# A two-block layer on one core: SBUF operands moved to PSUM, the head norm moved to VectorE, a second S5 buffer, a reordered opening, and each head's value product one tile later

## The chip, the cores and the metric

One NeuronCore of a Trainium2 chip runs the whole program. The time is the device time in microseconds (us). The kernel before took 3418.79 us, the median of three runs (3416.71 to 3423.25).

## What is computed

A residual stream `x` of 256 tokens by 2048 channels (f32) passes through two transformer blocks. The change touches the first block's token mixer alone:

```
mod = silu(c) @ w_ada + b_ada                       # shifts, scales, gates: 96 columns of 128
h = rmsnorm(x) * (1 + sc) + sh                      # the opening needs the first 32 columns
q, k, v, g_ret, u, gate_r, gate_s = split(h @ w_in)
q, k = rope(q), rope(k) * 128**-0.5                 # 8 heads, q and k of 128, v of 256
scores = (q k^T) * decay                            # causal, 256 x 256 per head
ret = head_group_norm(scores v)                     # mean and variance over the 256 of a head
y_ret = (silu(g_ret) * ret) @ w_ret_out
y_ssm = gelu(s5(u))                                 # 64 groups, complex diagonal scan over time
y = sigmoid(gate_r) * y_ret + sigmoid(gate_s) * glu(y_ssm @ w_s5_glu)
```

## The kernel before, in words

Everything is laid out feature by token: a tile is 128 features by 256 tokens. A matrix product of the first mixer takes one **weight tile** (128 output features, 16 slices of 128 by 128) and makes 48 matmuls of 256 columns, three for each slice (high part of the weights times high and low part of the activations, low part times high part: L636 to L638). Four ring slots hold weight tiles. SyncE loads the raw tile when the slot is free (L554), ScalarE copies it to the high part (L1006), VectorE subtracts for the low part (L1490, `split_lo`), TensorE multiplies. `ahead` on ScalarE and VectorE handles the tile two products ahead. Every engine works through its queue in the order of the code.

The stages that matter, in order of time:

- **Opening** (`modulation_rows`, `value_weights`, `row_pair`, `heads_values`). For each of the 16 channel tiles k VectorE reduces two rows of `w_ada`, 1 MB each (shift row k and scale row 16 + k, L1512), forms `normed`, and ScalarE adds the shift. TensorE then makes 16 matmuls of 512 columns (L730) that accumulate the values of all heads in all eight PSUM banks. SyncE issues the loads: value weights for two k at a time (2 MB in 8 loads, runs of 1 KB), then the rows of these two k.
- **u** (8 weight tiles, products of `u`).
- **heads** (32 weight tiles, four per head: q, k and the two halves of the gate; r is the tile's place in the head, n counts heads). Beside each tile run steps of the head before. After tile r = 0 TensorE makes the head's **value product** `ret_values` (scores times v, L753 to L755), for which VectorE must have masked the scores (`ret_masked`, L1750). At r = 1 VectorE takes the statistics of `p_o` and ScalarE the root; at r = 2 VectorE computes scale and shift (`ret_scale`, L1743, L1744), ScalarE writes the normed head (`ret_normed`, L1172), VectorE rotates q and k (`rotate`, L1763 to L1768). At r = 3 TensorE makes the scores of the new head and transposes the normed one (`ret_back`, L761), and ScalarE copies the gate product out of PSUM (`ret_g`). In the next head's r = 0 VectorE multiplies by the gate (`ret_out`, L1723), gates (`ret_gated`, L1755) and splits (`ret_done`, L1729).
- **ret** (32 weight tiles, four iterations g of eight, m = 0 to 7). For m of 0 to 3 ScalarE evacuates a gate; for m of 4 to 7 it copies the product to `val_a` or `val_b`, and VectorE multiplies it into `m_ret` (L1830). The first iteration also carries the last head's steps. From the second on VectorE reduces a late row of `w_ada` at m = 0, 3 and 6 (`aside_z`).
- **S5** runs through heads and ret: at every even m TensorE makes a product into `p_z`; one tile later VectorE turns it (L1696, L1697), adds (L1699, L1700) and scans twice (L1702, L1703) in `s5_w`; GpSimd turns it back (L2215 to L2218) into `s5_x`. VectorE waits with a new tile until GpSimd has finished the one before (`scan_done`).
- glu, out1 and the second half (feed-forward, second block) follow, and are not touched.

Of the kernel before, what the change touches and what calls it, by code (L numbers as in the profile page):

```python
# [137 lines left out]
def stages():  # L138
# [3 lines left out]
    ph["heads"] = Phase(4, [(W, KT)] * 8, 0)  # L142
    for name in ("u", "ffa", "att"):
        ph[name].opens = True
        ph[name].opening_lo = 4 if name == "u" else 3
# [56 lines left out]
def program(nc, dram, out):  # L202
    stored, ph = schedule(), stages()
    with ExitStack() as ctx:
# [13 lines left out]
        with ExitStack() as shared:  # L218
# [3 lines left out]
            s5_w = sb(shared, "s5_w", [P, 2, T])  # L222
            s5_v = sb(shared, "s5_v", [P, 2, T])
# [22 lines left out]
        with ExitStack() as block1:  # L246
            c_act = sb(block1, "c_act", [P, D])
            with ExitStack() as mixer:
# [42 lines left out]
                with ExitStack() as retention:  # L291
                    aside_r = sb(retention, "aside_r", [P, D])
                    qk_sin = sb(retention, "qk_sin", [P, 2, T])
                    qk_rot = sb(retention, "qk_rot", [P, 2, T])
                    g_t = sb(retention, "g_t", [P, 2, T])
# [5 lines left out]
                    gn_shift = sb(retention, "gn_shift", [P, 2])  # L301
# [90 lines left out]
        def bank(name):  # L392
# [3 lines left out]
        p_turn, p_score, p_o, p_norm, p_z, p_y = (bank(n) for n in ("p_turn", "p_score", "p_o", "p_norm", "p_z", "p_y"))  # L396
        v_banks = acc + [p_turn, p_score, p_o, p_norm, p_z, p_y]
# [29 lines left out]
        R = {n: sem("ret_" + n) for n in ("qk", "rope", "g", "decay", "scored", "masked", "gated", "summed", "var",  # L427
                                          "std", "scale", "normed", "back", "tanh", "out", "hi", "done")}
# [81 lines left out]
        def _(sp):  # L510
# [10 lines left out]
            def modulation_rows(k):  # L521

                for j, row in enumerate((k, KT + k)):
# [6 lines left out]
            def value_weights(two):  # L530

                quad, part = divmod(two, 2)
                if two == 2:
                    sp.wait_ge(c_set, 1)
                if quad >= 2:
                    sp.wait_ge(v_step, 4 * (quad - 2) + 2 * part + 2)
                for n in range(4):
                    for half in range(2):
                        at = stored["heads"].offsets[V_BLOCK[n // 2]]
                        src = dram["w_heads"][2 * (n % 2) + half, at:at + 2 * KT * P * P].rearrange(  # L540
                            "(j p c) -> p j c", j=2, p=P)[:, :, 2 * P * two:2 * P * (two + 1)]
                        dst = wv[quad % 2][n][:, 2 * half:2 * half + 2, 2 * part:2 * part + 2, :].rearrange("p j k c -> p j (k c)")
                        sp.dma_start(dst, src).then_inc(wv_in[quad % 2][part], 16)  # L543

            modulation_rows(0)
            for two in range(KT // 2):
                value_weights(two)
# [1859 lines left out]
```

## Time and profile before

| | |
|---|---|
| median of 3 runs | 3418.79 us |
| lowest, highest | 3416.71, 3423.25 us |
| the profiled execution, its own time | 3422.44 us |
| its span in the trace | 3420.7 us |
| mean granted TensorE clock | 0.99 |
| busy: TensorE, VectorE, ScalarE, GpSimd | 97%, 69%, 43%, 13% of the span |

Busy shares are means over stages with different limits. How to read the sections below: a row of a timeline gives the start and the duration in us, the engine and line, what is written and read, and in square brackets how long the engine sat idle before it and what ended that. A matmul's duration runs past the start of the next one, since matmuls are pipelined; the start to start distance is what one costs.

### The profile page before, as it was taken

To read this page: it belongs to the slowest core of one execution; us is meant where nothing else is said; L and a number is where in the kernel's file an instruction comes from. 1 tells how busy PE (TensorE), PEld (TensorE's weight loads), DVE (VectorE), ACT (ScalarE), POOL (GpSimd) and SP (SyncE) were. 2 spreads that over 40 slices of the span, in tenths; PEclk is the share of its full clock that TensorE was granted. 3 is DMA by queue.
4 is the path that set the end of the run, shared out by engine and by line. 5 is a ranking of instruction groups with operands and counts; after the bars stand their busy time and mean duration, and the time that the engine had idled before them with its cause. 6 is when DMAs were issued, how large, how long until landed. Compare 5 with 4: busy or idle time off the path is not lost.

```text
span 3420.7 us, 52032 instructions
## 1 busy us (share of the span) xinstructions
PE 3321.5 (97%) x20368; PEld 2945.6 (86%) x20368; DVE 2356.8 (69%) x2479; ACT 1469.3 (43%) x1504; POOL 431.8 (13%) x309
## 2 busy tenths in 40 slices
PE   7999999999989999999989999999999999999998
PEld 3599999899978888888878888888888888888887
DVE  6689988877676666656666567657677766666554
ACT  2256565444444444433354443443434444444332
POOL 1036677700200000000000000000002100000000
PEclk9999999999999999999999999999999999999999
DMA  9874455578735555567724444555555555555554
GB/s 380 346 306 173 165 184 216 203 302 307 265 134 186 194 185 193 186 246 265 259 99 169 164 162 180 187 185 190 186 194 190 185 193 187 190 190 182 192 190 147
DMA packets 126274, 706.34 MB, mean 206 GB/s; under 512 B 14160, under 2 KB 41424, under 8 KB 47840
## 3 DMA queue, kind: packets, MB, share of 16 engines
q1 hardware_dynamic: 115808, 695.96, 55.1%
q10 hardware_dynamic: 10368, 9.02, 0.8%
q8 instruction: 68, 1.11, 0.1%
q14 instruction: 30, 0.25, 0.0%
HBM read 702.83 MB, written 2.10 MB: 206 GB/s over the span
## 4 chain that ended last, share of the span: by engine, by line
PE 82%; DVE 8%; DMA 2%; POOL 2%; issue 2%; SPq 2%; ACT 1%; DVEq 0%; ACTq 0%; POOLq 0%
PE acc L639 44%; PE acc L640 24%; PE acc L636 4%; PE acc L638 4%; PE acc L637 4%; DVE ring_lo L1490 2%; SPq L543 1%; DVE ring_raw L1512 1%; DMA ring_raw<-w_ada 1%; DMA s_c_sb<-s_c 1%; POOL s_x L2215 1%; POOL s_w L2216 1%; PE p_norm L685 1%; ACT ring_hi L1006 0%; POOL s_prod L2225 0%
## 5 line engine op out<-in xcount | busy, mean ns | idle before, releaser
L639 PE MATMUL acc<-h_split,ring_hi 128*128 128x512 f32 x4736 | 1656.0, 392 | 9.2 <-DVE h_split L1552 4.5
L1490 DVE TENSOR_TENSOR ring_lo<-ring_raw,ring_hi 128x2048 fp32r<-128x2048 f32 (+2 forms) x560 | 1266.2, 2263 | 545.2 <-ACT ring_hi L1006 544.4
L640 PE MATMUL acc<-h_split,ring_lo 128*128 128x256 f32 x4736 | 1337.6, 282 | 0.0
L1006 ACT ACTIVATE ring_hi<-ring_raw 128x2048 fp32r<-128x2048 f32 (+2 forms) x560 | 1040.0, 1861 | 410.2 <-DMA ring_raw<-w_down 150.4
L639 PEld LDWEIGHTS acc<-h_split,ring_hi 128*128 128x128 f32 x4736 | 891.8, 188 | 197.4 <-issue 9.7
L640 PEld LDWEIGHTS acc<-h_split,ring_lo 128*128 128x128 f32 x4736 | 897.9, 190 | 0.4
L639 PE MATMUL acc<-ffn_split,ring_hi 128*128 128x512 f32 x1408 | 488.2, 390 | 0.0
L2157 POOL TENSOR_TENSOR sq_sum<-sq_sum,tile 128x256 f32<-128x256 f32 x60 | 76.5, 1275 | 2570.6 <-ACT tile L1032 2570.6
L640 PE MATMUL acc<-ffn_split,ring_lo 128*128 128x256 f32 x1408 | 397.1, 282 | 0.0
L636 PE MATMUL acc<-h_split,ring_hi 128*128 128x256 f32 x1152 | 329.9, 286 | 10.4 <-DVE ring_lo L1490 7.5
L637 PE MATMUL acc<-h_split,ring_hi 128*128 128x256 f32 x1152 | 323.8, 281 | 0.0
L638 PE MATMUL acc<-h_split,ring_lo 128*128 128x256 f32 x1152 | 323.6, 281 | 0.0
L639 PEld LDWEIGHTS acc<-ffn_split,ring_hi 128*128 128x128 f32 x1408 | 264.3, 188 | 55.4
L640 PEld LDWEIGHTS acc<-ffn_split,ring_lo 128*128 128x128 f32 x1408 | 266.1, 189 | 0.0
L636 PEld LDWEIGHTS acc<-h_split,ring_hi 128*128 128x128 f32 x1152 | 218.9, 190 | 13.2 <-issue 6.5
L637 PEld LDWEIGHTS acc<-h_split,ring_hi 128*128 128x128 f32 x1152 | 218.8, 190 | 0.8 <-issue 0.2
L638 PEld LDWEIGHTS acc<-h_split,ring_lo 128*128 128x128 f32 x1152 | 218.8, 190 | 0.0
L1323 ACT ACTIVATE ffn_split<-ffn_a 128x256 f32 (+1 forms) x88 | 36.8, 419 | 361.8 <-DVE ffn_a L1914 361.8
L1505 DVE TENSOR_REDUCE ffn_b<-acc 128x256 f32<-128x512 f32 x88 | 60.8, 691 | 144.1 <-PE acc L640 144.0
L1032 ACT ACTIVATE tile<-x_res 128x256 f32 (+1 forms) x80 | 33.0, 417 | 152.1 <-DVE x_res L2138 84.7
L2215 POOL TENSOR_TENSOR s_x<-s_w,s_tab 128x512 f32<-128x512 f32 x32 | 88.5, 2765 | 53.0 <-DVE s_w L1703 50.1
L1321 ACT ACTIVATE ffn_t<-ffn_a 128x256 f32<-128x256 f32 x88 | 36.8, 418 | 130.0 <-DVE ffn_a L1910 119.3
(384 smaller groups left out, 3993.1 us busy)
## 6 DMA issues: line engine op xcount, KB each, us to landing
ring_raw<-w_ff SPq DMA_DIRECT2D x88, 1024.0 KB, 4.8
ring_raw<-w_down SPq DMA_DIRECT2D x64, 1024.0 KB, 4.8
ring_raw<-w_ffb SPq DMA_DIRECT2D x56, 1024.0 KB, 4.8
ring_raw<-w_mix SPq DMA_DIRECT2D x48, 1024.0 KB, 4.8
ring_raw<-w_ada SPq DMA_DIRECT2D x32, 1024.0 KB, 10.8
ring_raw<-w_heads SPq DMA_DIRECT2D x32, 1024.0 KB, 4.8
ring_raw<-w_ret SPq DMA_DIRECT2D x32, 1024.0 KB, 5.2
ring_raw<-w_glu SPq DMA_DIRECT2D x32, 1024.0 KB, 5.0
```

The source lines that it names most:

```text
L636: mm(dst[:, 0:T], hi[s][:, t, :], moving[:, k, 0:T], start=start, stop=False)
L637: mm(dst[:, 0:T], hi[s][:, t, :], moving[:, k, T:], start=False, stop=False)
L638: return mm(dst[:, 0:T], lo[s][:, t, :], moving[:, k, 0:T], start=False, stop=stop)
L639: mm(dst[:], hi[s][:, t, :], moving[:, k, :], start=start, stop=False, skip_group_check=True)
L640: return mm(dst[:, T:], lo[s][:, t, :], moving[:, k, 0:T], start=False, stop=stop, skip_group_check=True)
L1006: run(hi[s][:, 0:n, :], raw[s][:, 0:n, :], COPY).then_inc(hi_done, 1)
L1321: run(t[i % 2][:], a[i % 2][:], ACT.Tanh, scale=0.5).then_inc(f_tanh, 1)
L1323: run(dst[:, 4 * g + (first + i), 0:T], a[i % 2][:], COPY, scale=0.5).then_inc(f_hi, 1)
L1490: tt(lo[s][:, 0:n, :], raw[s][:, 0:n, :], hi[s][:, 0:n, :], SUB).then_inc(lo_done, 1)
L1505: v.tensor_reduce(dst, acc[o % 2][:].rearrange("p (c t) -> p t c", c=2), AX_X, ADD).then_inc(sum_done, 1)
L2157: tt(sq_sum[:], sq_sum[:], tile[b][:], ALU.add).then_inc(sq_used, 1)
L2215: tt(xs[:], s5_w[:], sin, ALU.mult)
```

## The change

1. **PSUM operands.** `qk_sin` (the rotated part, then each head's gated result) moves from SBUF to the bank of `p_turn`. The copy `g_t` of the gate product disappears: ScalarE's Tanh and VectorE's `ret_gated` read the product's bank, and TensorE waits for `gated` where it waited for the copy. In S5 the second turned product is written in place in `p_z`, and `s5_v` disappears. In ret the products m = 4 to 7 are read by VectorE in their bank; ScalarE's copy to `val_a`, `val_b` disappears, and a new function `ret_bank` makes TensorE wait for VectorE (`m_done`) before it reuses such a bank.
2. **Norm.** VectorE writes the normed head (subtract the mean, multiply by the inverse root) in two operations, in place of its small shift operation and ScalarE's two.
3. **S5 buffers.** `s5_w` is doubled; VectorE waits for the tile before the last.
4. **One tile later.** `ret_values` goes from r = 0 to r = 1, the statistics and the root from r = 1 to r = 2, the norm from r = 2 to r = 3.
5. **Opening.** Value weights are loaded for four k at a time (runs of 2 KB) and for the last four k in two loads of two; the scale row comes before the shift row; `normed` is formed between the two rows.

```
-                for j, row in enumerate((k, KT + k)):
+                for j, row in enumerate((KT + k, k)):
...
-            for two in range(KT // 2):
-                value_weights(two)
-                for k in range(max(1, 2 * two), 2 * two + 2):
+            for first, n in ((0, 4), (4, 4), (8, 4), (12, 2), (14, 2)):
+                value_weights(first, n)
+                for k in range(max(1, first), first + n):
                     modulation_rows(k)
...
-                    pe.wait_ge(*((R["g"], n) if some(n) else (evac_done, ph["u"].outs * ph["u"].iters)))
+                    pe.wait_ge(*((R["gated"], n) if some(n) else (evac_done, ph["u"].outs * ph["u"].iters)))
...
-                    if r == 0 and some(n):
+                    if r == 1 and some(n):
                         ret_values(n, n - 1)
...
+            def ret_bank(p, g, m):
+
+                if 2 <= m < 6:
+                    return evac_done, p.out_count(g, m - 2)
+                if opening(g) and m < 2:
+                    return (R["gated"] if m else R["qk"]), HEADS
+                return m_done, 4 * g + (m - 1 if m < 2 else m - 5)
...
-            def row_pair(k):
-
-                p, first = ph["ada"], 2 * (k % 2)
-                for j in (first, first + 1):
-                    ada(raw[j][:].rearrange("p k c -> p (k c)"), raw_in[j], slot_free[j], p.uses(k // 2, j), j)
-                for j in (first, first + 1):
-                    dve.wait_ge(slot_free[j], p.uses(k // 2, j))
-                at = slice(k, k + KT + 1, KT)
-                own.step(stt(mod[:, at], ada_sum[:, first:first + 2], 0.5, b_ada[:, at], MUL, ADD))
-                own.step(stt(gain[:, 0, k:k + 1], mod[:, KT + k:KT + k + 1], 1.0, gains[:, 0, k:k + 1], ADD, MUL))
+            def first_row(k, j, at):
+
+                p, slot = ph["ada"], 2 * (k % 2) + j
+                ada(raw[slot][:].rearrange("p k c -> p (k c)"), raw_in[slot], slot_free[slot], p.uses(k // 2, slot), slot)
+                dve.wait_ge(slot_free[slot], p.uses(k // 2, slot))
+                return stt(mod[:, at:at + 1], ada_sum[:, slot:slot + 1], 0.5, b_ada[:, at:at + 1], MUL, ADD)
...
             for k in range(KT):
-                row_pair(k)
+                own.step(first_row(k, 0, KT + k))
+                own.step(stt(gain[:, 0, k:k + 1], mod[:, KT + k:KT + k + 1], 1.0, gains[:, 0, k:k + 1], ADD, MUL))
                 if k == 0:
                     inverse_std(1)
-                stt(normed[:, k, T:], x[:, k, :], gain[:, 0, k:k + 1], rstd[:], MUL, MUL).then_inc(n_done, 1)
+                own.step(stt(normed[:, k, T:], x[:, k, :], gain[:, 0, k:k + 1], rstd[:], MUL, MUL))
+                first_row(k, 1, k).then_inc(n_done, 1)
...
-                    if not isinstance(s, int) or s >= 1:
-                        dve.wait_ge(scan_done, s)
+                    if not isinstance(s, int) or s >= 2:
+                        dve.wait_ge(scan_done, s - 1)
                     cos, sin = waves_of(i)
-                    z = p_z[:].rearrange("p (c t) -> p c t", c=2)
-                    tt(s5_w[:], z, cos, MUL)
-                    tt(s5_v[:], z, sin, MUL).then_inc(z_used, 1)
+                    w, z = s5_w[i % 2], p_z[:].rearrange("p (c t) -> p c t", c=2)
+                    tt(w[:], z, cos, MUL)
+                    own.step(tt(z, z, sin, MUL))
+                    tt(w[:, 0, :], w[:, 0, :], z[:, 1, :], ADD)
+                    tt(w[:, 1, :], w[:, 1, :], z[:, 0, :], SUB).then_inc(z_used, 1)
...
-            def ret_scale(n):
+            def ret_normed(n):
 
                 dve.wait_ge(R["std"], n)
                 own.step(v.reciprocal(gn_mean[:, :, 1], gn_mean[:, :, 1]))
-                stt(gn_shift[:], gn_mean[:, :, 0], -1.0, gn_mean[:, :, 1], MUL, MUL).then_inc(R["scale"], 1)
+                for s in range(2):
+                    ins = v.tensor_scalar(o_t[:, s, :], p_o[:, s * T:(s + 1) * T], gn_mean[:, s, 0:1], gn_mean[:, s, 1:2], SUB, MUL)
+                ins.then_inc(R["normed"], 1)
...
-                stt(g_act[:], g_act[:], 1.0, g_t[:], ADD, MUL).then_inc(R["gated"], 1)
+                gate_bank = acc[1][:].rearrange("p (j t) -> p j t", j=2)
+                stt(g_act[:], g_act[:], 1.0, gate_bank, ADD, MUL).then_inc(R["gated"], 1)
...
-                        evacuated(p, g, m)
-                        stt(m_ret[:, d, :], m_ret[:, d, :], 1.0, (val_a, val_b)[m % 2][:], ADD, MUL).then_inc(m_done, 1)
+                        dve.wait_ge(slot_free[m % SLOTS], p.uses(g, m))
+                        dve.wait_ge(evac_done, p.out_count(g, m - 4))
+                        stt(m_ret[:, d, :], m_ret[:, d, :], 1.0, acc[m % 2][:, 0:T], ADD, MUL).then_inc(m_done, 1)
```

## Rows read from the trace of the kernel before

**Rows 1.** Busy time by stage: stretch, length, each engine's busy us (instructions), clock, DMA share, GB/s
```profile
26.00:155.00 129.00, 117.33 (x257) 50.69 (x258) 96.62 (x145) 25.09 (x47) 17.31 (x18) 0.95 1.00 382
...
206.00:443.00 237.00, 220.64 (x1711) 213.90 (x1710) 224.60 (x266) 143.26 (x162) 152.92 (x107) 0.99 0.51 186
443.00:690.00 247.00, 234.25 (x1825) 227.89 (x1825) 210.42 (x205) 129.10 (x142) 180.63 (x117) 0.98 0.54 201
```
**Rows 2.** Waits of TensorE in heads: who <- for whom: us in all, times, longest
```profile
PE p_o L753 <- DVE scores L1750: 13.8, 7, 3.9
```
**Rows 3.** Waits of TensorE in ret and the start of glu
```profile
PE acc L636 <- DVE ring_lo L1490: 10.2, 7, 2.6
...
PE acc L636 <- DVE ret_split L1729: 1.8, 1, 1.8
```
**Rows 4.** Timeline of TensorE over one head: start, us, what, idle before
```profile
317.77 0.37 PE L636 MATMUL acc<-h_split,ring_hi 128*128 128x256 f32 x1
...
325.68 0.69 PE L753 MATMUL p_o<-v_heads,scores 128*128 x2 [2.06 <-DVE scores L1750]
...
347.99 0.60 PE L761 MATMUL p_norm<-ident,o_t 128*128 128x128 f32 x4
348.34 0.37 PE L636 MATMUL acc<-h_split,ring_hi 128*128 128x256 f32 x1
...
356.26 0.69 PE L753 MATMUL p_o<-v_heads,scores 128*128 x2 [2.06 <-DVE scores L1750]
```
**Rows 5.** Timeline of VectorE around that head's end and in the next head
```profile
349.37 0.69 DVE L1696 TENSOR_TENSOR s_w<-p_z,s_tab 128x512 f32<-128x512 f32 x1
...
354.96 0.68 DVE L1723 TENSOR_TENSOR qk_sin<-p_norm,g_act 128x512 f32<-128x512 f32 x1
355.56 0.55 DVE L1750 SCALAR_TENSOR_TENSOR scores<-p_score,scores 128x384 f32<-128x384 f32 x1
...
359.00 1.77 DVE L1755 SCALAR_TENSOR_TENSOR g_act<-g_act,g_t 128x512 f32<-128x512 f32 x1
...
378.39 0.68 DVE L1696 TENSOR_TENSOR s_w<-p_z,s_tab 128x512 f32<-128x512 f32 x1
```
**Rows 6.** Timeline of GpSimd at the same time
```profile
356.88 3.34 POOL L2216 TENSOR_TENSOR s_w<-s_w,s_tab 128x512 f32<-128x512 f32 x1
```
**Rows 7.** VectorE by line: least, median, greatest ns, first and last start, shapes
```profile
L1696 DVE TENSOR_TENSOR s_w<-p_z,s_tab x32: 677/692/693, 210.8 to 671.6; 128x512 f32<-128x512 f32 x32
...
L1768 DVE TENSOR_TENSOR qk_rot<-qk_rot,qk_sin x8: 693/1242/1270, 218.4 to 436.1; 128x512 f32<-128x512 f32 x8
...
L1744 DVE SCALAR_TENSOR_TENSOR gn_shift<-gn_mean x8: 1041/1052/1057, 248.4 to 460.3; 128x2 f32<-128x2 f32 x8
...
L1755 DVE SCALAR_TENSOR_TENSOR g_act<-g_act,g_t x8: 1750/1764/1772, 237.3 to 450.6; 128x512 f32<-128x512 f32 x8
...
L1711 DVE SCALAR_TENSOR_TENSOR s_y<-u,s_d_sb,p_y x8: 468/468/482, 284.5 to 690.4; 128x256 f32<-128x256 f32 x8
...
L1713 DVE TENSOR_SCALAR s_g<-s_g x8: 293/295/428, 285.5 to 691.4; 128x256 f32<-128x256 f32 x8
...
L1830 DVE SCALAR_TENSOR_TENSOR m_ret<-m_ret,val_b x8: 542/1505/1516, 489.0 to 677.2; 128x256 f32 x6, 128x256 f32<-128x256 f32 x2
```
**Rows 8.** Busy time of the second, third and fourth iteration of ret (columns as rows 1)
```profile
501.00:553.50 52.50, 52.27 (x419) 51.09 (x418) 42.68 (x40) 30.04 (x33) 39.34 (x26) 1.00 0.55 201
553.50:610.70 57.20, 53.53 (x418) 51.93 (x417) 50.16 (x49) 30.15 (x33) 44.85 (x29) 0.97 0.56 220
610.70:668.60 57.90, 54.23 (x420) 52.70 (x419) 51.03 (x50) 27.15 (x29) 45.06 (x28) 0.97 0.61 233
```
**Rows 9.** Opening: TensorE's waits in all; two stretches with their DMA (columns as rows 1)
```profile
PE acc L730 <- ACT normed L1093: 15.0, 5, 5.9
...
17.30:24.50 7.20, 5.01 (x19) 2.52 (x17) 3.81 (x5) 3.76 (x9) 0.00 (x0) 1.00 1.08 352
38.00:45.50 7.50, 4.97 (x11) 1.95 (x11) 7.12 (x9) 0.93 (x2) 0.00 (x0) 0.93 1.01 409
```

More of the change, by code:

```diff
@@ L221, in program @@
             s5_sin = sb(shared, "s5_sin", [P, 2, T])
-            s5_w = sb(shared, "s5_w", [P, 2, T])
-            s5_v = sb(shared, "s5_v", [P, 2, T])
+            s5_w = [sb(shared, f"s5_w{i}", [P, 2, T]) for i in range(2)]
         x = sb(ctx, "x_res", [P, KT, T])
@@ L425, in program @@
             sem(n) for n in ("s5_y_done", "s5_sq", "s5_in", "s5_tanh", "s5_m", "s5_hi", "s5_done"))
-        R = {n: sem("ret_" + n) for n in ("qk", "rope", "g", "decay", "scored", "masked", "gated", "summed", "var",
-                                          "std", "scale", "normed", "back", "tanh", "out", "hi", "done")}
+        R = {n: sem("ret_" + n) for n in ("qk", "rope", "decay", "scored", "masked", "gated", "summed", "var", "std",
+                                          "normed", "back", "tanh", "out", "hi", "done")}
         A = {n: sem("att_" + n) for n in ("turned", "scored", "v_n", "max", "exp", "p", "p_turned", "p_t", "summed",
@@ L802, in _ @@
                         last = (R["done"], HEADS, 2)
-                    product(p, g, m, [(m, 0, 16, ret_flat if m >= 4 else h, 0)], last)
+                    product(p, g, m, [(m, 0, 16, ret_flat if m >= 4 else h, 0)], last, ret_bank(p, g, m))
                     if opening(g) and m == 0:
@@ L1167, in ret_std @@
                 run(gn_mean[:, :, 1], gn_mean[:, :, 1], ACT.Sqrt, bias=eps[:, 1:2]).then_inc(R["std"], 1)
-            def ret_normed(n):
-                act.wait_ge(R["scale"], n)
-                for s in range(2):
-                    ins = run(o_t[:, s, :], p_o[:, s * T:(s + 1) * T], ACT.Identity, bias=gn_shift[:, s:s + 1],
-                              scale=gn_mean[:, s, 1:2])
-                ins.then_inc(R["normed"], 1)
             def ret_decay(n):
@@ L2213, in turned_on @@
                 cos, sin = (s5_tab[i // 2][:, c, i % 2, :].unsqueeze(1).to_broadcast([P, 2, T]) for c in range(2))
-                xs = s5_x[i % 2]
-                tt(xs[:], s5_w[:], sin, ALU.mult)
-                own.step(tt(s5_w[:], s5_w[:], cos, ALU.mult))
-                tt(xs[:, 1, :], s5_w[:, 0, :], xs[:, 1, :], ALU.subtract)
-                tt(xs[:, 0, :], xs[:, 0, :], s5_w[:, 1, :], ALU.add).then_inc(scan_done, 1)
+                xs, w = s5_x[i % 2], s5_w[i % 2]
+                tt(xs[:], w[:], sin, ALU.mult)
+                own.step(tt(w[:], w[:], cos, ALU.mult))
+                tt(xs[:, 1, :], w[:, 0, :], xs[:, 1, :], ALU.subtract)
+                tt(xs[:, 0, :], xs[:, 0, :], w[:, 1, :], ALU.add).then_inc(scan_done, 1)
             def c_scaled(i, s, uses):
```

99 lines of the change are left out of this document (42 added, 57 removed).

## The prediction, as it was put on record before the changed kernel ran

> **What bounds the kernel now.** I read four views in this order. First the busy time by stage [rows 1]: TensorE is busy nearly all the time everywhere, so only its gaps and the rate at which work reaches it can be won. In heads and ret VectorE is busy 224.6 of 237.0 and 210.4 of 247.0 us: a second engine close to full. Second, TensorE's own waits: in heads all of them are one place, the value product that waits for the masked scores, 13.8 us in seven waits [rows 2]; in ret they are the low halves of weight tiles, 10.2 us in seven, and the last split of the normed heads, 1.8 us [rows 3]. In the opening TensorE waits 15.0 us for `normed` in five places [rows 9]. Third, the timelines, for why VectorE is late [rows 4 to 6]. TensorE starts a head at 348.34, finishes its first tile and stands from 354.20 to 356.26. VectorE masks only at 355.56; it is not waiting, it is behind. One reason is GpSimd: the gate operation at 359.00 takes 1.77 us and ends 0.55 us after GpSimd's operation of 356.88 + 3.34 = 360.22. Fourth, durations by line [rows 7]: an operation of 512 columns with both inputs in SBUF takes 0.693 us when it is lucky and 1.242 as a rule; with one input in PSUM it takes 0.677 to 0.693, in all 32 cases, though GpSimd worked through much of that time. The shift of two columns takes 1.05 us, which is waiting and not work.
>
> From that I take the mechanism: VectorE and GpSimd hold each other up when both read SBUF in this way, and operations with a PSUM input are out of it.
>
> **The change part by part, heads.** Durations are of the profiled execution (3422.44 us, 3.7 above the median); savings are subtracted from the median.
>
> The value product's wait. From one value product to the next is 356.26 - 325.68 = 30.58 us; less the wait of 2.06 and the 0.16 by which matmuls otherwise overlap, a full head is 28.4 us. One tile is 354.20 - 348.34 = 5.9 us, so the small products take the remaining 5 us or so and the second tile ends some 13 us after the head's start (bounds 11.8 and 16.8). The masked scores were ready at 355.56 + 0.55 - 348.34 = 7.8 us. Moved one tile later, the product has over 4 us of slack: all seven waits go, 13.8 + 7 x 0.16 = 14.9 us.
>
> What is late next. VectorE's new duties in order of risk: (a) the normed head, needed by the transposes 347.99 - 317.77 - 2.2 = 28.0 us after the head's start. VectorE today begins its tile-3 work at 349.37 - 317.77 = 31.6 us in an even head and 378.39 - 348.34 = 30.1 in an odd one [rows 4, 5], later than that. So this only works if VectorE moves up. (b) The gate: TensorE's third tile now waits for `gated`, at about 14.5 us; VectorE ended it at 359.00 + 1.77 - 348.34 = 12.4 us, which fits.
>
> How far VectorE moves up, for each head: gate operation 1.76 to 0.69, the rotation's add 1.24 to 0.69, the split after the gate, also 512 columns with two SBUF inputs, the same 0.55 [rows 7]: 1.07 + 0.55 + 0.55. S5's first add of each of two tiles loses some waiting, 0 to 0.3 us each, say 0.3 in all. The shift goes (1.05) and two subtract-and-multiply operations of 256 columns from PSUM come: the nearest rows are 0.295 (scalar operation, SBUF) and 0.468 (three operands, PSUM), so 0.59 to 0.94; I take 0.7, nearer the first, as there is one tensor input. Net 2.8 us (2.2 to 3.2). A pair of heads holds VectorE today for nearly all of its 61.1 us; it becomes about 55.5 against 56.8 on TensorE. From the order of the code the queue also gains its masking and gating about 1.7 us earlier within the head, and it no longer stands for `scan_done`. It therefore catches up within a head or two; then (a) is met with some 2 us to spare. The first pair also carries the reductions of extra rows of `w_ada`, where I leave 1.5 us of stall. Heads: 14.9 - 1.5 = **13.4 us** (10 to 14.9). ScalarE loses copies only, and its root and exponentials a tile later lie beside tiles; they cost nothing, as ScalarE is busy 143 of 237 us [rows 1].
>
> **Ret.** The second iteration has hardly a stall: 52.5 us; the third and fourth take 57.2 and 57.9 [rows 8], so stalls and the slow clock after them cost 4.7 + 5.4 = 10.1 us. What goes: `m_ret` 1.505 us becomes at most 0.47 (rows 7, 256 columns with a PSUM input), up to 4 us for each iteration, and GpSimd's hold on `s5_w`. What comes: the bank is freed by VectorE, behind its queue. Products 4 to 7 are awaited in order, so VectorE stands at each and its work is bunched at m = 6, 7 and 0. Bounds: nothing of 10.1 if VectorE stays as late as now, all of it if not; I take 85%, since 4 us less work for each iteration nearly equals the loss, 8.6 us. In the first iteration the split (1.8 us) and the last head's steps give 1.5. At the start of glu ScalarE waits for the last `m_ret`, and two of the seven waits of rows 3 lie there; I take 2.0. Ret in all: **12.1 us** (4 to 16).
>
> **Opening.** Value weights came at 352 GB/s, rows of `w_ada` at 409 [rows 9]; 12.6 MB now come in runs of twice the length. If the loss lies in the number of runs, four sevenths of the difference to runs of 8 KB is won: (12.6 / 0.352 - 12.6 / 0.409) x 0.57 = 2.8 us. But the end of the stage is TensorE's: 16 k of 16 matmuls, with 15.0 us of waits. The first product now needs 4.2 MB of value weights, not 2.1, and starts about 3 us later. The rows of k = 1 to 3 then come without weights between them, so the third wait group and its slow restart go (about 4.5 us), and the late waits shrink by the 2.8 us. Against -3.0 that leaves 4.3; I take **4.2 us** (-3 to 7). The longest wait, 5.9 us at k = 4, stands behind S5's angles on VectorE and stays. The scale row first, `normed` between the rows: the sum of VectorE's work is the same, so nothing.
>
> **A page that speaks against it.** By rows 7 a PSUM operand costs nothing (0.692 with it, 0.693 at best without). The Trainium skill's page "VectorE: DVE Perf Modes", section "The TRN2 errata", charges a PSUM source 120 cycles where an SBUF source costs 58. By that, as an estimate, some 14 operations a head would each be 0.065 us dearer, 0.9 us a head; VectorE would still gain, and the sum would lose about 1 us in the first pair. The trace does not agree with it.
>
> **Sum.** 13.4 + 12.1 + 4.2 = 29.7 us; 3418.8 - 29.7 = **3389 us**. After glu's start nothing changes.
>
> **The rivals.**
> - *VectorE keeps its place* (slower). If its lateness comes from its order and its waits for products, not from the load, the normed head is ready at 31.6 + 0.9 and 30.1 + 0.9 us against 28.0: 4.5 + 3.0 us for each pair against 4.4 removed, +3 for each pair, +10.5 over three and a half. The banks of ret then come late at m = 5 and 7 too, some 1.4 us twice in three iterations, +8. With an opening that gives 4 that is 3418.8 + 10.5 + 8 - 4 = 3433 us. It decides from the point where VectorE begins tile 3 later than 27 us after the head's start. Against it: 5.6 us less work for a pair. Chance 0.06.
> - *Contention moves rather than goes.* GpSimd runs on, and the remaining operations with two SBUF inputs (low halves, scans, reductions) meet it more often. VectorE gains only half, and heads give 6, ret 3, opening 2: 3408 us. For it: a low half takes longer whenever it meets GpSimd. Chance 0.09.
> - *Banks of ret.* VectorE's queue at m = 6 to 0 holds TensorE back by about 2 us for each iteration; ret gives 5 and not 12: 3396 us. Chance 0.13.
> - *The opening gives nothing or loses 2*, because the first quad is late and VectorE follows: 3394 us. Chance 0.12.
> - *As forecast*, 3383 to 3393: 0.60.
>
> The range takes all but the first rival and most of the second: **3377 to 3406**; its lower end is everything won (14.9 + 16 + 7 = 38, plus the spread of the runs). A measurement of this kernel tells about 0.2% (7 us) from no change: faster than 3412 is 0.91, within 0.03, slower 0.06.
>
> **What would show it.** In heads: no wait before the value product, a full head of 28.4 us, the gate operation at 0.7 us; the transposes without a wait after the first pair. If they wait for VectorE's normed head, the first rival is at work. In ret: `m_ret` under 0.5 us, iterations under 53.5 us; a wait of a product for `m_ret` is the third rival. In the opening: the first value product near 29 us, the last near 151 and not 155. The prediction is wrong if two-input operations from PSUM take much over 0.7 us, or if GpSimd, which now gets its tiles earlier, holds up the low halves more than it does now.

## The result, and the profile after

The changed kernel takes 3382.53 us (median of 4 runs, 3381.48 to 3389.52), the kernel before, run beside it, 3420.57 us: a ratio of 0.9894, with a 95% interval of 0.9877 to 0.9911. That is 38.0 us faster. The forecast was 3389 us, 29.7 us faster. A later set of runs of the same kernel gave 3382.83 us and a ratio of 0.9884 (0.9869 to 0.9900); where the experiments below give a distance to the changed kernel, it is to this median.

The profiled execution took 3381.64 us (span 3379.9), 40.8 us less than that of before. The stages, by the end of the last matmul of each:

| stage | before | after | gain | forecast |
|---|---|---|---|---|
| opening, to the last value product | 155.1 | 154.7 | 0.5 | 4.2 |
| heads, first S5 product to last scores | 234.1 | 217.4 | 16.7 | 13.4 |
| ret and glu's start, to the last S5 product | 250.6 | 229.9 | 20.7 | 12.1 |
| products with `y_ssm` | 161.4 | 162.0 | -0.6 | 0 |
| out1 (products with `merged`) | 92.0 | 88.7 | 3.3 | 0 |
| all behind it | 2476.9 | 2476.7 | 0.2 | 0 |

The stretch of `u`, between the opening and heads, takes 50.6 us in both.

Busy time by stage, with the columns of [rows 1]; the stretches end where the stages of after end:

```profile
30.00:155.00 125.00, 116.03 (x261) 50.75 (x262) 99.79 (x161) 24.79 (x46) 17.74 (x18) 0.95 0.98 381
206.00:423.00 217.00, 216.64 (x1709) 211.87 (x1708) 203.23 (x275) 135.21 (x142) 152.83 (x109) 1.00 0.54 199
423.00:653.00 230.00, 228.91 (x1833) 224.82 (x1833) 196.57 (x205) 120.55 (x122) 180.58 (x114) 1.00 0.60 219
```

TensorE stood 16.4 us in heads and 12.8 in ret before (the first of these stretches ended at 443 us, so it holds the 2.6 us with which ret began); now it is 0.4 and 1.1 us. VectorE's busy time fell by 21.4 and 13.8 us. TensorE's waits in heads, and in ret with glu's start, each have one row, where [rows 2, 3] had 13.8, 10.2 and 1.8:

```profile
PE p_norm L765 <- DVE o_t L1730: 0.4, 1, 0.4
...
PE acc L635 <- DVE ret_split L1714: 1.1, 1, 1.1
```

The second to fourth iteration of ret, beside [rows 8] (52.5, 57.2, 57.9 us):

```profile
477.80:529.70 51.90, 51.90 (x418) 51.06 (x417) 43.93 (x44) 26.92 (x28) 40.09 (x26) 1.00 0.57 206
529.70:581.90 52.20, 52.20 (x418) 51.17 (x417) 47.49 (x48) 28.82 (x29) 45.77 (x28) 1.00 0.63 239
581.90:633.90 52.00, 52.00 (x419) 51.16 (x418) 47.53 (x49) 24.54 (x23) 44.11 (x27) 1.00 0.69 260
```

VectorE's operations by line in heads and ret (out<-in, shapes, count, busy us, mean ns of one, idle before them), beside [rows 7]:

```profile
L1682 DVE TENSOR_TENSOR p_z<-p_z,s_tab 128x512 f32<-128x512 f32 x32 | 22.1, 689 | 0.1
...
L1730 DVE TENSOR_SCALAR o_t<-p_o,gn_mean 128x256 f32<-128x256 f32 x16 | 8.0, 540 | 0.3
...
L1756 DVE TENSOR_TENSOR qk_rot<-qk_rot,p_turn 128x512 f32<-128x512 f32 x8 | 5.5, 687 | 0.3
L1743 DVE SCALAR_TENSOR_TENSOR g_act<-g_act,acc 128x512 f32<-128x512 f32 x8 | 5.4, 673 | 0.0
...
L1819 DVE SCALAR_TENSOR_TENSOR m_ret<-m_ret,acc 128x256 f32 x12 | 4.9, 409 | 0.0
```

The gate operation went from 1.764 to 0.673 us, the rotation's add from 1.242 to 0.687. For `m_ret` the prediction took 1.505 us before; that is the median of the half of these operations that [rows 7] shows. The other half was shorter:

```profile
L1830 DVE SCALAR_TENSOR_TENSOR m_ret<-m_ret,val_a x8: 732/959/1512, 482.4 to 667.3; 128x256 f32 x6, 128x256 f32<-128x256 f32 x2
```

All sixteen together went from 19.2 to 6.5 us, which is 3.2 us for each iteration; the prediction allowed up to 4. The two halves of the normed head start 0.5 us apart (540 ns each), 1.0 us together.

The opening is the part that did not do as forecast. TensorE's waits there, beside the 15.0 us of [rows 9], add up to 16.1:

```profile
PE acc L734 <- ACT normed L1104: 8.8, 3, 6.6
PE acc L734 <- DMA wv_a<-w_heads: 7.3, 1, 7.3
```

### The profile page after: what moved, and what is told of

Read it like the earlier page. It is cut to its first block, busy times and chain, and to the rows that moved or that the text cites. A ratio compares the mean times of both kernels' runs of the same rounds, so it can differ in the third digit from the quotient of the medians.

```text
span 3379.9 us, 51972 instructions
## 1 busy us (share of the span) xinstructions
PE 3307.3 (98%) x20368; PEld 2937.2 (87%) x20368; DVE 2324.5 (69%) x2503; ACT 1452.4 (43%) x1464; POOL 435.2 (13%) x309
## 4 chain that ended last, share of the span: by engine, by line
PE 90%; DVE 5%; ACT 1%; DMA 1%; SPq 1%; issue 1%; DVEq 0%; ACTq 0%
PE acc L638 45%; PE acc L639 24%; PE acc L635 6%; PE acc L636 6%; PE acc L637 6%; DVE ring_raw L1499 1%; DVE ring_lo L1477 1%; DMA ring_raw<-w_ada 1%; SPq L542 1%; PE p_y L705 1%; PE p_norm L687 1%; PE p_z L715 1%; ACT ring_hi L1017 0%; DMA ring_raw<-w_out 0%; DVE rstd L1524 0%
## 5 line engine op out<-in xcount | busy, mean ns | idle before, releaser
L2204 POOL TENSOR_TENSOR s_x<-s_w,s_tab 128x512 f32<-128x512 f32 x32 | 86.6, 2707 | 29.9 <-DVE s_w L1688 29.8
```

Source lines behind the costliest of these rows:

```text
L2204: tt(xs[:], w[:], sin, ALU.mult)
```

## The experiments

Eleven altered kernels ran, and the changed kernel once more: 1 to 4, 5 to 8 and 9 to 12, each group beside its own runs of the kernel before (medians 3420.87, 3422.07 and 3420.83 us). Ratios are to those. The stages below are measured in the traces, as in the table above.

**1. The shift alone, on the kernel before.**

```diff
-                    if r == 0 and some(n):
+                    if r == 1 and some(n):
                         ret_values(n, n - 1)
...
-                    elif r == 1 and some(n):
-                        ret_stats(n)
                     elif r == 2:
                         if some(n):
-                            ret_scale(n)
+                            ret_stats(n)
                         rotate(p, g, m - 1, n)
+                    elif r == 3 and some(n):
+                        ret_scale(n)
```

(and ScalarE's root at `r == 2`, its normed head at `r == 3`.)

> The kernel before with one part of the change alone: in heads the value product runs after the head's second tile, the statistics and the root at the third, shift and normed head at the fourth. All operands stay in SBUF, S5 and ret as before. Theory 'load' (VectorE's work paces the heads, wherever TensorE asks for it): VectorE takes up a head's fourth-tile work 30 to 31.6 us after the head's start, the transposes are due at 28.0, so the waits of 2 us for each head move from the value product to the transposes and heads gain 0 to 3 us: 3416 to 3421 us, ratio 0.999 to 1.000. Theory 'place' (the value product was asked for too early, the load is no matter): no wait of either kind, a head of 28.4 us, heads gain 13 to 15 us, about 3406 us, ratio 0.996. The pitch of out1's matmuls: 117.8 ns if it belongs to what is in the other stages of the changed kernel.

Measured: 3414.62 us, ratio 0.998 (0.997 to 0.999). Heads take 228.2 us, 5.8 less than before, and the waits are in another place:

```profile
PE p_norm L761 <- ACT o_t L1172: 6.7, 5, 4.7
```

Neither theory holds as it was put. Of the 13.8 us before the value product 6.7 come back before the transposes, 4.7 of them in the first pair; after it a head takes 28.4 to 29.5 us from one value product to the next, not 30.6. Ret takes 249.1 us, 1.5 less than before.

**2. The changed kernel with the shift undone.** 

```diff
-                    if r == 1 and some(n):
+                    if r == 0 and some(n):
                         ret_values(n, n - 1)
...
+                    elif r == 1 and some(n):
+                        ret_stats(n)
                     elif r == 2:
                         if some(n):
-                            ret_stats(n)
+                            ret_normed(n)
                         rotate(p, g, m - 1, n)
-                    elif r == 3 and some(n):
-                        ret_normed(n)
```

(and ScalarE's root at `r == 1`.)

> The changed kernel with the value product back after the first tile (statistics and root at the second, normed head at the third), all PSUM operands, S5 buffers, ret and opening kept. In the changed kernel the masked scores were ready 342.40 + 0.55 - 338.06 = 4.9 us after a head's start, before its first tile ends (5.7). Theory 'load': no wait comes back, or under 3 us in all: 3383 to 3386 us, ratio 0.989 to 0.990. Theory 'place': the seven waits of 2 us come back: about 3396 us, ratio 0.993.

Measured: 3388.99 us, 0.9903 (0.9887 to 0.9920). Heads take 219.3 us, 14.7 less than before:

```profile
PE p_o L757 <- DVE scores L1737: 2.1, 2, 1.2
```

The waits of 2 us don't come back; there are two, at the first two value products, and after the second a head takes 28.3 to 28.4 us, as in the changed kernel. So for the steady heads the load was enough: an early value product costs nothing once VectorE is lighter. The stage is 1.2 to 2.0 us longer than in the two traces of the changed kernel, but that is no measure of the shift: seven traces of kernels whose instructions in heads are those of the changed kernel (runs 3, 4, 5, 7, 8, 12 and its first trace) lie between 217.2 and 220.9 us. The median is 6.2 us above that of the changed kernel; the rest of it is not in heads, and the traces put it in no stage for certain: `y_ssm` and out1, whose instructions are the same, together take 4.8 us more here than in the first trace of the changed kernel and 1.3 more than in the second.

**3. The changed kernel with the opening of before.**

```diff
-            for first, n in ((0, 4), (4, 4), (8, 4), (12, 2), (14, 2)):
-                value_weights(first, n)
-                for k in range(max(1, first), first + n):
+            for two in range(KT // 2):
+                value_weights(two)
+                for k in range(max(1, 2 * two), 2 * two + 2):
                     modulation_rows(k)
...
-                own.step(first_row(k, 0, KT + k))
...
+                row_pair(k)
```

> The changed kernel with the opening of the kernel before (value weights in eight parts with rows between them, both rows of w_ada before the first normed tile). Heads, ret and all else as changed. If the opening gave nothing, as the ends of the value products say (155.14 before, 154.66 after): 3382 to 3384 us, ratio 0.989 to 0.990, and the waits before normed are again 3.5, 2.5, 5.9, 1.1 and 2.0 us. If it gave the 4.2 us of the forecast in a place that I have not seen: about 3387 us, 0.9905. Out1's pitch stays at 113.3 ns if it does not hang on the opening's instructions, and returns to 117.8 if it does.

Measured: 3386.15 us, 0.9900 (0.9883 to 0.9916), 3 us above the changed kernel, which the intervals don't tell from none. The last value product ends at 155.0 us (154.7 and 154.0 in the two traces of the changed kernel). The first head's transposes wait 2.0 us, against 0.4 and 1.1 in the two traces of the changed kernel.

**4. The changed kernel with ScalarE's copies for `m_ret` restored.**

```diff
-                        dve.wait_ge(slot_free[m % SLOTS], p.uses(g, m))
-                        dve.wait_ge(evac_done, p.out_count(g, m - 4))
-                        stt(m_ret[:, d, :], m_ret[:, d, :], 1.0, acc[m % 2][:, 0:T], ADD, MUL).then_inc(m_done, 1)
+                        evacuated(p, g, m)
+                        stt(m_ret[:, d, :], m_ret[:, d, :], 1.0, (val_a, val_b)[m % 2][:], ADD, MUL).then_inc(m_done, 1)
```

(and ScalarE's copies, and TensorE's waits for the banks of ret, as before.)

> The changed kernel with ScalarE's copies of ret's second products back in SBUF (val_a, val_b), m_ret made from them, and the banks freed by the copies as before. Theory 'work of ret' (the gain of ret comes from m_ret of 0.5 instead of 1.5 us): later iterations take 56 to 58 us again, ret loses 8 to 10 us, about 3391 us, ratio 0.992. Theory 'inherited' (VectorE came late into ret from heads, and S5's operands and the shorter heads gave the gain): ret loses 0 to 3 us, 3383 to 3386, ratio 0.989 to 0.990.

Measured: 3393.11 us, 0.9916 (0.9899 to 0.9932), 10 us above the changed kernel. Ret and glu's start take 238.1 us, 8.3 more, and the waits for low halves are there again:

```profile
PE acc L634 <- DVE ring_lo L1478: 5.4, 6, 1.8
```

"Work of ret" holds. It is 8.3 of the 20.7 us (4.7 in the second to fourth iteration, 3.6 in glu's start, none in the first iteration), so 12.4 had to come from elsewhere.

**5. The changed kernel once more.**

> The changed kernel, unaltered, run again: it stands beside the other kernels of this call, and shows what belongs to an execution and what to the program. In the first trace of it out1's matmuls took 88.67 us from the end of the y_ssm products (91.99 in the kernel before, and 87.4, 91.4, 92.0 and 91.9 in the four kernels tried), and the first head waited 0.36 us before its transposes (1.99 and 2.30 in two kernels that differ only outside heads). If these belong to the program they return to within 0.3 us; if to the execution, out1 comes out anywhere between 87 and 92 us and the wait between 0.3 and 2.3. Time 3381 to 3387 us, ratio 0.989 to 0.990.

Measured: 3382.83 us, 0.9884 (0.9869 to 0.9900). Out1 takes 91.9 us, as before the change, and the first head waits 1.1. So the 3.3 us of out1 in the table belong to that execution and not to the program. The span of this trace is 3381.5 us, with heads at 218.2 and ret at 229.8: the gains of heads and ret repeat within 0.8 us.

**6. The changed kernel with S5 as before.**

```diff
-            s5_w = [sb(shared, f"s5_w{i}", [P, 2, T]) for i in range(2)]
+            s5_w = sb(shared, "s5_w", [P, 2, T])
+            s5_v = sb(shared, "s5_v", [P, 2, T])
...
-                    if not isinstance(s, int) or s >= 2:
-                        dve.wait_ge(scan_done, s - 1)
+                    if not isinstance(s, int) or s >= 1:
+                        dve.wait_ge(scan_done, s)
...
-                    own.step(tt(z, z, sin, MUL))
+                    tt(s5_v[:], z, sin, MUL).then_inc(z_used, 1)
```

> The changed kernel with S5's part as before: one s5_w, the second product in s5_v in SBUF, scan_done of the tile before awaited. Ret gained 20.7 us, of which the run with ScalarE's copies restored gave back 8.3 and the start of ret some 4; about 8 us are open. Theory 's5' (VectorE stood behind GpSimd's hold on s5_w, or its adds from SBUF were held up by it): ret loses 5 to 9 us, heads 1 to 4, about 3391 to 3395 us, ratio 0.992. Rival 'inherited' (VectorE is ahead because heads handed it over in time): ret loses under 2 us, 3383 to 3387, ratio 0.989 to 0.990.

Measured: 3399.63 us, 0.9936 (0.9921 to 0.9952), 16.8 us above the changed kernel and more than either theory had. Ret loses 9.5 us, heads 3.0; the heads' loss is in the first pair, and within the spread named under run 2. VectorE's idle time, by line, in heads and ret (the last two columns: idle us, and whom it ended with):

```profile
L1682 DVE TENSOR_TENSOR s_w<-p_z,s_tab 128x512 f32<-128x512 f32 x32 | 22.0, 687 | 25.6 <-POOL s_x L2208 25.6
...
L1685 DVE TENSOR_TENSOR s_w<-s_w,s_v 128x256 f32<-128x256 f32 x32 | 17.3, 539 | 1.1
```

25.6 us is what VectorE stood for GpSimd. And TensorE's waits in ret have a name that neither the kernel before nor the changed one shows:

```profile
PE acc L636 <- DVE m_ret L1820: 6.3, 5, 1.6
```

**7 and 8. The block for S5's angles spread over six k; in 8 also the first quad of value weights in two halves.** `s5_angles` was made a generator with five `yield`s; the second hunk is in 8 only:

```diff
-                if k == 3:
-                    s5_angles()
+                if k >= 3:
+                    next(angles, None)
...
-            for first, n in ((0, 4), (4, 4), (8, 4), (12, 2), (14, 2)):
+            for first, n in ((0, 2), (2, 2), (4, 4), (8, 4), (12, 2), (14, 2)):
```

> The changed kernel with VectorE's block for S5's angles (52.5 to 60.1 us, with 2.2 us of waiting ahead of it, between k = 3 and k = 4) cut into six pieces, one behind each of k = 3 to 8. Theory 'queue runs dry' (the longer runs of the value weights save about 3 us by 60 us, but the rows behind the block are issued late, and 366 and 379 GB/s in 60 to 92 us give it back): the wait at k = 4 falls from 6.6 us to about 4, GB/s between 60 and 92 us stay over 400, the last row of w_ada lands near 138.5 instead of 141.8, and the last value product ends near 151 instead of 154.7; 3 to 4 us faster than the changed kernel, ratio 0.9885. Rival (bandwidth is what it is, the longer runs give nothing): the last row lands at 141 to 142, the time is that of the changed kernel.

> As the kernel with the angles spread, and the first quad of value weights loaded as two halves of 1 KB runs, so that the first value product again needs 2.1 MB and starts near 26 instead of 30 us. If the end of the stage hangs on the last row of w_ada, the earlier start gives nothing and the shorter runs cost about 1 us: as the other within 1 us. If it hangs on TensorE's sum of work and waits, 2 to 4 us faster than the other: ratio 0.9875.

Measured: 3390.08 us (0.9904, 0.9889 to 0.9920) and 3392.33 us (0.9915, 0.9902 to 0.9929), 7 and 10 us above the changed kernel. Both theories are left untested, since the edit did something else. In the first of the two (21.1 us in the second, in place of the 20.4):

```profile
ACT s_r L1082 <- DVE s_t L1589: 20.4, 1, 20.4
...
PE acc L734 <- ACT normed L1104: 15.3, 1, 15.3
```

ScalarE waits for `s5_params` behind its work for k = 3. I had moved the operation that sets it behind two more k of VectorE's rows. Behind ScalarE's wait stands the bias of `normed` for k = 4, and behind that TensorE.

**9. The changed kernel with one `s5_w`, the second product still in `p_z`.**

```diff
-                    if not isinstance(s, int) or s >= 2:
-                        dve.wait_ge(scan_done, s - 1)
+                    if not isinstance(s, int) or s >= 1:
+                        dve.wait_ge(scan_done, s)
...
-                    w, z = s5_w[i % 2], p_z[:].rearrange("p (c t) -> p c t", c=2)
+                    w, z = s5_w[0], p_z[:].rearrange("p (c t) -> p c t", c=2)
```

> The changed kernel with a single s5_w (VectorE waits for GpSimd's operations on the tile before), the second product still in p_z. With all of S5 as before, the kernel lost 15.5 us of span, and VectorE waited for GpSimd's s_x 9.3 us in heads and 15.2 in ret. Theory 'one buffer' (the wait for GpSimd is the whole of it): these waits are back, ret loses 8 to 9.5 us and heads 2 to 4, 3395 to 3400 us, ratio 0.993. Theory 'operand' (the adds from SBUF beside GpSimd cost it): the waits are under 5 us in all, 3383 to 3387 us, ratio 0.989 to 0.990.

Measured: 3395.28 us, 0.9924 (0.9907 to 0.9940), 12.5 us above the changed kernel:

```profile
L1681 DVE TENSOR_TENSOR s_w<-p_z,s_tab 128x512 f32<-128x512 f32 x32 | 22.0, 687 | 29.2 <-POOL s_x L2207 28.2 <-PE p_z L715 1.0
...
L1683 DVE TENSOR_TENSOR s_w<-s_w,p_z 128x256 f32<-128x256 f32 x32 | 13.5, 421 | 1.1
```

"One buffer" holds. The wait is all there (28.2 us), though the adds are at their short 421 ns. By the medians the buffer is 12.5 of S5's 16.8 us. The other 4 us are not shown to be the operands': they lie within the intervals of the two ratios, and heads and ret together take 460.0 us here (heads 222.7, ret 237.2), 460.5 in run 6 and 448.0 in the changed kernel. So in these stages the buffer is the whole loss. The operands spare VectorE 7.6 us (539 and 533 ns against 421 and 414 for 64 adds) and TensorE next to nothing, once the wait for GpSimd is there.

**10. The S5 part alone, on the kernel before.** 

```diff
-            s5_w = sb(shared, "s5_w", [P, 2, T])
-            s5_v = sb(shared, "s5_v", [P, 2, T])
+            s5_w = [sb(shared, f"s5_w{i}", [P, 2, T]) for i in range(2)]
...
-                    if not isinstance(s, int) or s >= 1:
-                        dve.wait_ge(scan_done, s)
+                    if not isinstance(s, int) or s >= 2:
+                        dve.wait_ge(scan_done, s - 1)
...
-                    tt(s5_v[:], z, sin, MUL).then_inc(z_used, 1)
+                    own.step(tt(z, z, sin, MUL))
```

> The kernel before with the change's S5 part alone (two s5_w, the second product in p_z). In the kernel before VectorE waited for GpSimd's s_x 2.8 us in heads and 11.7 in ret. If the parts add up, it gains what its removal lost: ret 8 to 10 us, heads 3 to 6, about 3407 us, ratio 0.996. If each part only counts once the others have brought VectorE forward (m_ret of 1.5 us and the early value product hold TensorE anyway), it gains under 5 us: 3415 to 3420, ratio 0.999.

Measured: 3406.35 us, 0.9959 (0.9945 to 0.9973), 14.5 us faster than the kernel before. Heads gain 5.1 us, ret 8.2. TensorE's waits in heads, then in ret:

```profile
PE p_o L752 <- DVE scores L1749: 8.9, 6, 2.1
...
PE acc L635 <- DVE ring_lo L1489: 4.6, 5, 1.7
PE acc L635 <- issue: 2.6, 1, 2.6
```

The part gives about as much alone (14.5) as its removal takes (16.8): this part does not need the others. The heads still take 29.8 to 30.6 us each, so it is not what brings them to 28.3. TensorE's wait of 2.6 us without a releaser, which ret begins with, stays.

**11. The changed kernel with the normed head back on ScalarE.**

```diff
-                for s in range(2):
-                    ins = v.tensor_scalar(o_t[:, s, :], p_o[:, s * T:(s + 1) * T], gn_mean[:, s, 0:1], gn_mean[:, s, 1:2], SUB, MUL)
-                ins.then_inc(R["normed"], 1)
+                stt(gn_shift[:], gn_mean[:, :, 0], -1.0, gn_mean[:, :, 1], MUL, MUL).then_inc(R["scale"], 1)
```

(and `ret_normed` on ScalarE, with two scaled copies at `r == 3`.)

> The changed kernel with the normed head back on ScalarE (shift on VectorE, two scaled copies on ScalarE, both at the fourth tile). VectorE gives 1.00 us and takes back a shift of 1.05, so its load is the same; the chain to the transposes gets ScalarE's queue in it. If that queue is short, as its 143 busy of 237 us say: within 2 us of the changed kernel, 3381 to 3386. If ScalarE stands behind its high halves and gelu steps there, the transposes wait 0.5 to 1 us for each head: 3386 to 3391, ratio 0.991.

Measured: 3386.77 us, 0.9899 (0.9882 to 0.9915), 4 us above the changed kernel, just outside the first expectation. The time lies in the range of the second, but not for its reason. Heads take 3.4 to 4.2 us more, and it is one wait in the first head and not one in each:

```profile
PE p_norm L765 <- ACT o_t L1183: 3.1, 1, 3.1
```

The first head waits 2.0 to 2.3 us in runs 3, 4, 7 and 8 too, where VectorE writes the normed head, and 3.4 in run 9. So it is not shown that moving the norm to VectorE gained anything beyond this spread; from the second head on it made no difference (28.3 us either way).

**12. The angles in three pieces, with the one that ScalarE waits for left in place.**

```diff
                 v.reciprocal(t[6], t[6]).then_inc(s5_params, 1)
+                yield
                 own.step(v.tensor_tensor_scan(s5_step[:], ones[:, 0:RAMP], ones[:, 0:RAMP], -1.0, MUL, ADD))
...
+                yield
                 half_op(s5_round[:], s5_turn[:], ROUND, ADD)
```

(and ScalarE's exponential one k earlier.)

> The changed kernel with the block for S5's angles cut so that nobody stands behind it: the piece up to s5_params (2.7 us), for which ScalarE's queue waits, stays behind k = 3, the steps come behind k = 4 and the rounding behind k = 5, and ScalarE's exponential goes one k earlier, so that VectorE doesn't wait 2.2 us for it. The first try at this cut the piece that ScalarE waits for, and ScalarE stood 20.4 us. Theory 'queue runs dry': VectorE is free for the row of k = 4 when it lands, the wait at k = 4 falls from 6 us to 3 or 4, the last row of w_ada lands at 139 to 140 instead of 141.8, the last value product ends at 151.5 to 153 instead of 154 to 154.7: 1 to 3 us faster than the changed kernel, ratio 0.988. Rival (the end hangs on the rate of the transfers alone): last row at 141 to 142, no difference.

Measured: 3385.75 us, 0.9896 (0.9879 to 0.9912), not faster than the changed kernel. The wait at k = 4 fell to 4.6 us, but one of 1.3 us came at 82 us and the one at 98 us was 2.2 (0.7 and 1.7 in the two traces of the changed kernel); the last row of `w_ada` landed at 142.1 us and the last value product ended at 155.0. The stretch that I had put down to the angles, in the changed kernel and then here (columns as rows 1):

```profile
60.00:78.00 18.00, 11.41 (x21) 4.94 (x22) 17.48 (x27) 1.85 (x4) 14.24 (x14) 0.81 0.95 366
```

```profile
60.00:78.00 18.00, 13.42 (x28) 5.82 (x28) 17.31 (x32) 1.85 (x4) 4.43 (x5) 0.91 0.94 361
```

The rate is 361 GB/s, where it was 366. Cutting the block up brought neither the rate back nor the end of the stage forward. It does not clear the angles altogether: in the changed kernel the block ended at 60.1 us, ahead of this stretch, and here two of the three pieces lie inside it (from 64.5 and 72.9 us), so VectorE is as full as it was (17.3 of 18 us, then 17.5).

## Why the prediction was right or wrong

**Heads: right in place and cause, 3.3 us too low (2.5 by the second trace), and wrong in what it gave to the shift.** All seven waits before the value product went; from one value product to the next it is 28.3 us (forecast 28.4); the gate operation takes 0.67 us (0.7), the normed head 1.0 (0.7). The transposes wait once, in the first pair. The sum was 14.9 - 1.5. What it lacked is the slow restart: after the 3.9 us wait of the kernel before, the granted clock over the next 4.5 us was 0.62 and the next small products took 4.6 us instead of the 2.8 that they take without a wait, so that wait cost 1.8 us more than it measured; and the residual stall was 0.4 (1.1 in the second trace), not 1.5. As to which part does it, the prediction gave the shift all of the 14.9 us and the lighter VectorE only the catching up. Run 1 gives the shift alone 5.8 us; run 2 gives everything but the shift 14.7, as much as kernels that have the shift give within their spread. So the lighter VectorE was the stronger part, and the shift was hardly needed beside it. Of the lighter VectorE's parts the norm (run 11) and S5 (runs 6 and 9) can be taken back and a steady head stays at 28.3 us; what is left by exclusion are the PSUM operands of the gate, its split and the rotation.

**Ret: right in sign, and every term too low.** The forecast split it as 8.6 (second to fourth iteration) + 1.5 (first) + 2.0 (glu's start) = 12.1. Measured: 11.3, 6.1 and 3.3. The largest miss is the first iteration, 4.6 us.

In the later iterations the mis-sized step is the work behind the stall. The prediction laid the lateness to `m_ret` and mentioned "GpSimd's hold on `s5_w`" without a price, and took 85% of 10.1 us. `m_ret` with its copies is worth 8.3 us of ret (run 4, 3.6 of them in glu's start, where 2.0 was forecast for everything), and S5's part 9.5 (run 6), of which the hold alone makes 7.4 (run 9). The hold's price could be read ahead of time, in a row of VectorE's own waits in ret that I didn't use:

```profile
DVE s_w L1696 <- POOL s_x L2218: 11.7, 7, 2.8
```

The heads have such a row too (2.8 us, one wait): 14.5 us in all, and the S5 part alone gave 14.5 us (run 10), though not stage by stage (5.1 in heads, 8.2 in ret). In heads VectorE was so late that GpSimd was mostly through by then, so the hold hardly showed (so I read it); with VectorE on time the wait grows, to 9.3 us in heads and some 16 in ret and glu's start (run 6, 25.6 in all). The time does not grow with it: run 6 loses 3.0 us in heads, and after the first pair a head still takes 28.3. The prediction said only that VectorE "no longer stands for `scan_done`".

Of the first iteration I had missed this, in TensorE's timeline of the kernel before:

```profile
442.83 0.35 PE L636 MATMUL acc<-h_split,ring_hi 128*128 128x256 f32 x1 [2.55 <-issue]
```

TensorE waited there for `R["g"]`, ScalarE's copy of the last head's gate. ScalarE's copy ran from 442.16 to 442.74 us. The change removes that wait: the product goes ahead and only the next bank waits for `gated`. "issue" names no releaser, and I took it for nothing. With the slower tile behind it (7.2 us at a granted clock of 0.76, instead of 5.7) that is 4.1 of the 6.1 us, as I read the trace. No run undid this part by itself; the wait stands in run 10, whose first iteration takes the 61 us of the kernel before, and is gone in run 4, whose first iteration takes 55.1 as in the changed kernel. In run 1 it is gone too, with VectorE as loaded as before, and the first iteration gains only 1.5 us; so the rest of the figure hangs on VectorE being on time.

**Opening: wrong, 0.5 us (1.2 in the second trace) where 4.2 was forecast.** The first product was at 30.2 us, the wait of 2.5 us at 44.4 us did go, the wait at k = 4 stayed (6.6). From the first product to the last value product it took 124.5 us instead of 129.0: the 4.5 us forecast for the wait group and its restart came, and the 4.0 us of the late start took them. The failed steps are two. The first wait is 7.3 us instead of 3.5, on the weights themselves, so the late start cost 4.0 us, not 3. And "the late waits shrink by the 2.8 us" did not happen: the last row of `w_ada` landed at 141.8 us, against 142.2. The longer runs did bring a higher rate while weights came (389 GB/s from 46.2 to 54.2 us, against 352 in [rows 9]), but over 60 to 78 and 78 to 92 us it was 366 and 379 against 389 and 399. My reading of that: in the new order eight rows come in one bunch, VectorE takes some 3.2 us for each (rows were issued at 62.5, 65.8, 68.6 and 71.9 us as their slots came free), a row transfers in 2.5, and the next weights stand behind them in SP's queue. Before, at most four rows stood between weights. Run 12 shows that cutting up the angles does not mend it; that it is the bunching is argued from the trace, since no kernel with more slots or another order ran.

**"After glu's start nothing changes": right.** The 3.3 us of out1 did not recur (run 5).

**The rivals.** *VectorE keeps its place* did not occur; run 1, where VectorE keeps its load, shows its mechanism, 4.7 of 6.7 us in the first pair. *Contention moves* did not occur: the low halves take 2524 ns on average over both stages, 2539 before, all sixteen reductions of late rows 44.7 us and 44.2 before, the scans 48.0 and 47.4. *Banks of ret* did not in the changed kernel, but it is a real mechanism: with VectorE late again, TensorE waited 6.3 us (run 6) and 5.1 (run 9) for `m_ret`. *The opening gives nothing* did occur, and the gain came in spite of it. That the time lies within 7 us of the forecast is in part luck: two terms were too low (by 3.3 and 8.6 us) and one too high (by 3.7). The first two alone would have put it at 3377 us, on the edge of the range.

The weighed rule of the Trainium skill, in "VectorE: DVE Perf Modes", section "The TRN2 errata", that a PSUM source has the higher fixed cost: the changed kernel has an operation with `p_z` as source and target at 689 ns, and the same shape from SBUF took 693 at best in the kernel before [rows 7]. The trace still does not show the charge.

**What stays open.** The PSUM operands of the gate and the rotation were not undone by themselves, nor was the new wait at the start of ret. Why the first head's wait varies between 0.2 and 2.3 us among kernels with the same instructions in heads is not settled, and it blurs every price of under 4 us there. And no version beat the changed kernel: runs 7, 8 and 12 tried to mend the opening and did not.

## What to carry to other kernels

When an engine is nearly full, list its own waits first: a wait for another engine's hold on a buffer (here GpSimd's on `s5_w`, 11.7 us in one stage) is load as much as work is, and a second buffer, at no instruction more, was the largest single part that was measured (12.5 us, run 9). The wait in the kernel as it stands was a fair price here (14.5 us waited, 14.5 gained by the S5 part alone); the longer wait that shows once the engine is on time (25.6 and 28.2 us in runs 6 and 9) was not, since part of it falls where nobody stands behind that engine. An edit that moves a signal must be followed to whoever waits for it and to what stands behind that wait, even where it is meant to help another engine (20.4 us of ScalarE in run 7).

## What the runs showed of the hardware

- One and the same program ran the same 768 matmuls of out1 in 88.7 us in one execution and in 91.9 in another, both at a granted clock of 1.00 (113.3 and 117.5 ns from one start to the next). Of the other traces only that of run 1 was near the faster pace (113.6 ns). A difference of 3 us in a stage whose instructions are untouched is no effect of a change.
- VectorE beside GpSimd: an add of 256 columns takes 421 ns with one input in PSUM and 539 on average with both in SBUF (runs 9 and 6), a gate of 512 columns 673 against 1764. In the kernel before all eight gate operations took 1.75 to 1.77 us, and each ended 0.55 us after the end of a GpSimd operation that it had begun beside. The Trainium skill's page "SBUF — State Buffer", section "Who interferes with whom", describes such a lock between the two engines, and the trace agrees.
- Value weights came at 389 GB/s in runs of 2 KB and at 352 in runs of 1 KB, but the opening's last row landed only 0.4 us earlier in all.
